# Expert weights ahead of the stage barrier, choice rounds moved, and a closing norm with ACT's square root, in an encoder kernel

## The reference

```python
tokens = rms_norm(x, norm_g).reshape(n_tok, d)
logits = jnp.einsum('nd,de->ne', tokens, w_router)
affinity = jax.nn.softmax(logits, axis=-1)
gate, idx = lax.top_k(affinity.T, cap)        # each of 16 experts takes 32 prompt, 128 sample tokens
xe = tokens[idx]
hid = silu(xe @ w_gate) * (xe @ w_up)         # per expert, 1024 x 1024 matrices
ye = (hid @ w_down) * gate
out = zeros.at[idx].add(ye)
y = rms_norm(x + out, final_g)
```

## Time and profile before

| | |
|---|---|
| median of 3 runs | 1362.23 us (1359.22, 1362.23, 1362.28) |
| the profiled execution | 1361.18 us, span 1359.5 us |
| TensorE busy | 1281.0 us, 94% |
| TensorE weight loads | 1116.0 us, 82% |
| VectorE busy | 916.3 us, 67% |
| ACT busy | 706.1 us, 52% |
| GpSimd busy | 306.1 us, 23% |
| mean granted TensorE clock | 0.969 |
| read from HBM, written | 274.41 MB, 39.44 MB |

### The profile page before, as it was taken

One profiled execution on the slowest core, in us unless ns is written; L12 is line 12 of the kernel. 1 busy time (PEld: TensorE's weight loads), 2 busy tenths in 40 slices (PEclk: granted clock), 3 DMA queues, 4 the chain that ended last, 5 costly groups with the idle time before them and its releaser, 6 DMA issues.

```text
span 1359.5 us, 24950 instructions
## 1 busy us (share of the span) xinstructions
PE 1281.0 (94%) x9744; PEld 1116.0 (82%) x9744; DVE 916.3 (67%) x1336; ACT 706.1 (52%) x1025; POOL 306.1 (23%) x304
## 2 busy tenths in 40 slices
PE   8999999999998999924999999999999999999992
PEld 7889999888897888814888888988898888988891
DVE  5363122341475555597988888888988888888976
ACT  6345221102244444215766677666766677666762
POOL 1122121010042222012141322223131322223030
PEclk8999999999999999966999999999999999999996
DMA  8022454342157774219799999999999999999994
GB/s 288 32 74 77 124 173 148 102 128 46 68 198 229 196 202 156 78 70 370 253 325 333 304 316 319 335 310 302 317 321 331 300 317 319 336 309 304 298 364 187
DMA packets 242030, 314.74 MB, mean 232 GB/s; under 512 B 16096, under 2 KB 206048, under 8 KB 241968
## 3 DMA queue, kind: packets, MB, share of 16 engines
q1 hardware_dynamic: 226576, 268.54, 59.9%
q0 software_dynamic: 15392, 45.36, 11.4%
HBM read 274.41 MB, written 39.44 MB: 231 GB/s over the span
## 4 chain that ended last, share of the span: by engine, by line
PE 90%; DVE 5%; DMA 2%; issue 1%; SPq 1%; ACT 1%; POOL 0%; ACTq 0%; DVEq 0%; POOLq 0%
PE psum L1860 26%; PE psum L1937 22%; PE psum L1944 10%; PE psum L1960 8%; PE psum L1750 7%; PE psum L1978 4%; PE psum L1969 4%; PE psum L1930 1%; PE psum L1783 1%; PE psum L1796 1%; PE psum L1797 1%; PE psum L1706 1%; PE psum L1731 1%; DVE eraw L1678 1%; DVE GI L1309 1%
## 5 line engine op out<-in xcount | busy, mean ns | idle before, releaser
L1609 DVE TENSOR_TENSOR elo<-eraw,ehi 128x2048 bf16<-128x2048 f32 x192 | 433.4, 2284 | 2.1 <-ACT ehi L1057 1.1
L1057 ACT ACTIVATE ehi<-eraw 128x2048 fp32r<-128x2048 f32 x192 | 362.3, 1902 | 48.4 <-DMA eraw<-in_w_gate_dram 28.9
L1937 PE MATMUL psum<-xc,ehi 128*128 128x320 f32 x2048 | 332.4, 314 | 1.9 <-DVE xc L1614 1.9
L1937 PEld LDWEIGHTS psum<-xc,ehi 128*128 128x128 f32 x2048 | 304.2, 189 | 3.5 <-DVE xc L1614 2.3
L1944 PE MATMUL psum<-xb,elo 128*128 128x160 bf16 x2048 | 164.1, 233 | 0.0
L1622 DVE TENSOR_REDUCE gu<-psum 128x320 f32<-128x640 f32 x128 | 105.2, 822 | 83.4 <-PE psum L1944 83.1
L1944 PEld LDWEIGHTS psum<-xb,elo 128*128 128x128 bf16 x2048 | 138.8, 98 | 13.2 <-issue 0.2
L1860 PE MATMUL psum<-hn_hi,whi 128*128 128x512 f32 (+1 forms) x384 | 137.3, 358 | 0.0
L1860 PE MATMUL psum<-hn_lo,whi 128*128 128x512 f32 (+1 forms) x384 | 136.1, 354 | 0.0
L1860 PE MATMUL psum<-hn_hi,wlo 128*128 128x512 f32 (+1 forms) x384 | 135.8, 354 | 0.0
L1960 PE MATMUL psum<-ehi,hc 128*128 128x512 f32 x512 | 132.6, 406 | 0.0
(11 more groups left out here) (253 smaller groups left out, 1978.8 us busy)
## 6 DMA issues: line engine op xcount, KB each, us to landing
eraw<-in_w_gate_dram SPq DMA_DIRECT2D x64, 1024.0 KB, 9.7
eraw<-in_w_up_dram SPq DMA_DIRECT2D x64, 1024.0 KB, 10.7
eraw<-in_w_down_dram SPq DMA_DIRECT2D x64, 1024.0 KB, 12.5
wraw<-in_w_in_dram SPq DMA_DIRECT2D x12, 1024.0 KB, 7.5
negm<-negm_d SPq DMA_DIRECT2D x10, 512.0 KB, 6.9
acc_d<-x POOLq DMA_DIRECT2D x10, 512.0 KB, 5.4
tok_d<-tk POOLq DMA_DIRECT2D x10, 512.0 KB, 3.0
v<-v_d SPq DMA_DIRECT2D x18, 256.0 KB, 4.3
```

The lines of the kernel that those rows point to most:

```text
L1057: act.activation(f["ehi"][:, j % RING, :], f["eraw"][:, raw_slot(s, j), :], ACT.Copy).then_inc(S["ehi"], 1)
L1609: dve.tensor_tensor(f["elo"][:, j % RING, :], f["eraw"][:, raw_slot(s, j), :], f["ehi"][:, j % RING, :].bitcast(F32), ALU.subtract).then_i ...
L1937: pe.matmul(o[:, 0:2 * NC], hi[:, k, c], x[:, k, :, :].rearrange("p a t -> p (a t)"), start=(k == 0), stop=False, skip_group_check=True)
```

## The change

- **Weights.** SP arrives at the barrier without waiting. The first expert's loads wait for the last output projection, and its down pieces (from piece 8 on, `RAW`) for the landing of the first gather's prompt part. That part now has its own semaphore `gath_p`, so the sample rows can be transposed before it lands.
- **Tokens of tile 7.** `LATE = NS - 1`: tile 7 now takes the way of tiles 8 and 9 over ACT and POOL. POOL starts these three multiplications when all ten affinity tiles are done. `g2b` has a place of its own, since the weights now land where it lay.
- **Choice rounds.** ACT copies the affinities to `AFF`. The rounds are laid 0, 1 to 3, 4 and 5, 6, 7, and then 8 to 11 after `arrive`.
- **Clock.** TensorE runs 48 transposes of the identity matrix after it has transposed the choice.
- **Closing norm.** For the second batch and for the last rows ACT takes the square root (with its table loaded by a first small root ahead of the second batch's sums), and VectorE forms the reciprocal and one Newton step (`polish`). Two of the second batch's six tiles are scaled after the last expert's rows are added. The prompt's last rows are finished and scattered first, waiting only for the prompt's plain stores, and the sample's second.

```diff
@@ -231,7 +231,7 @@
...
         d.update(overlay(at_stage, ("x1", [P, 2, D], F32)))
-        d.update(overlay(at_conv, ("tk", [P, 2, D], F32)))
+        d.update(overlay(at_conv, ("tk", [P, 2, D], F32), ("g2b", [P, D], F32)))
@@ -249,7 +249,7 @@
...
         og = d["og"][:, 2, SP_:T].rearrange("p (s n) -> p s n", s=2)
-        g2b = d["og"][:, 3, SP_:T]
+        g2b = d["g2b"][:, :]
@@ -294,8 +294,9 @@
...
         same_token = spare[:, 2 * D:2 * D + P]
-        fs = spare[:, 2 * D + P:2 * D + P + 3 * NT].rearrange("p (a n) -> p a n", a=3)
-        fl = spare[:, 2 * D + 2 * P:2 * D + 2 * P + 8].rearrange("p (a n) -> p a n", a=4)
+        fs = spare[:, 2 * D + P:2 * D + P + 4 * NT].rearrange("p (a n) -> p a n", a=4)
+        fl = spare[:, 2 * D + 2 * P:2 * D + 2 * P + 10].rearrange("p (a n) -> p a n", a=5)
+        eps = spare[:, 2 * D + 2 * P + 32:2 * D + 2 * P + 33]
         gains = colS[:, :, :].rearrange("p a c -> p (a c)")
@@ -381,6 +382,8 @@
...
+
+        LATE = NS - 1
@@ -546,9 +549,9 @@
...
             load_x(0)
-            sp.dma_start(g2b, rows_of(norm2_g)).then_inc(S["g2b_in"], 16)
             stored(staged[-1])
             load_mix(1)
+            sp.dma_start(g2b, rows_of(norm2_g)).then_inc(S["g2b_in"], 16)
             for n in range(2, NT + 1):
@@ -557,12 +560,18 @@
...
                     load_mix(n)
-            barrier(sp, 1)
+            arrive(sp)
...
                 for j in range(NB):
+                    if first and j == 0:
+
+                        sp.wait_ge(S["o_ps"], 2 * NT)
+                    if first and j == RAW:
+
+                        sp.wait_ge(S["gath_p"], 16)
                     if j >= RAW:
@@ -597,8 +606,8 @@
...
                 sp.wait_ge(S["f_y"], k + 1)
-                sp.dma_start(y_chunk[n], final_tile(n)).then_inc(S["f_out"], 16)
-            sp.wait_ge(S["f_out"], 16 * NT)
+                sp.dma_start(y_chunk[n], final_tile(n)).then_inc(S["f_out_p" if n < NTP else "f_out"], 16)
+            sp.wait_ge(S["f_out"], 16 * NS)
@@ -706,12 +715,13 @@
...
                     select_causal(n + 2)
-                if n >= 2 and not joint(m):
+                if n >= 2 and m < LATE:
                     pool.wait_ge(S["tk_done"], m + 1)
...
             pool.wait_ge(S["g2b_in"], 16)
-            for m in range(NS, NT):
-                pool.wait_ge(S["tk_scaled"], m - NS + 1)
+            pool.wait_ge(S["aff_done"], NT)
+            for m in range(LATE, NT):
+                pool.wait_ge(S["tk_scaled"], m - LATE + 1)
                 pool.tensor_tensor(d["tk"][:, m % 2, :], d["tk"][:, m % 2, :], g2b, ALU.mult
@@ -745,7 +755,7 @@
...
                                         bass.IndirectOffsetOnAxis(ap=idx[:, 1:2], axis=0)
-                                        ).then_inc(S["gath"], 16)
+                                        ).then_inc(S["gath_p"], 16)
@@ -792,6 +802,7 @@
...
                                     ).then_inc(S["f_gath"], 16)
+            pool.memset(eps, EPS)
             ch(pool.memset(same_token, 0.0))
@@ -801,15 +812,16 @@
...
             y_quarters = y_prompt[0].rearrange("t (j n) -> (t j) n", j=4)
-            pool.wait_ge(S["f_out"], 16 * NT)
+            pool.wait_ge(S["f_out_p"], 16 * NTP)
             pool.wait_ge(S["f_done"], 1)
+            settle()
+            pool.indirect_dma_start(y_quarters, bass.IndirectOffsetOnAxis(ap=f["idx"][:, 1, 1:2], axis=0),
+                                    f["yp"][:, :], None).then_inc(S["f_set"], 16)
+            pool.wait_ge(S["f_out"], 16 * NS)
+            pool.wait_ge(S["f_done"], 2)
             settle()
...
                                     f["yt"][:, :], None).then_inc(S["f_set"], 16)
-            pool.wait_ge(S["f_done"], 2)
-            settle()
-            pool.indirect_dma_start(y_quarters, bass.IndirectOffsetOnAxis(ap=f["idx"][:, 1, 1:2], axis=0),
-                                    f["yp"][:, :], None).then_inc(S["f_set"], 16)
             pool.wait_ge(S["f_set"], 32)
@@ -989,6 +1001,14 @@
...
+            def scaled_tokens(m):
+
+                act.wait_ge(tk_out[m % 2], 16 * (m // 2))
+                if not joint(m):
+                    act.wait_ge(S["lgmax"], m + 1)
+                act.activation(d["tk"][:, m % 2, :], d["x1"][:, m % 2, :], ACT.Copy, scale=d["ms"][:, m % 2, 1, H:H + 1]
+                               ).then_inc(S["tk_scaled"], 1)
+
@@ -1035,15 +1055,21 @@
...
                     columns_out(n - 1, 0)
+                if n == NT - 1:
+
+                    act.wait_ge(S["affT_ps"], 1)
+                    for i in range(NS // 4):
+                        act.activation(AFF[HALF2 * i:HALF2 * i + NE, :], psum[0:NE, (0, 4)[i], :], ACT.Copy
+                                       ).then_inc(S["aff_out"], 1)
                 if n < NT:
                     heads_high(n)
+                if n == NT - 1:
+                    scaled_tokens(LATE)
             for m in range(NS, NT):
...
             for m in range(NS, NT):
-                act.wait_ge(tk_out[m % 2], 16 * (m // 2))
-                act.activation(d["tk"][:, m % 2, :], d["x1"][:, m % 2, :], ACT.Copy, scale=d["ms"][:, m % 2, 1, H:H + 1]
-                               ).then_inc(S["tk_scaled"], 1)
-            barrier(act, 1)
+                scaled_tokens(m)
+            arrive(act)
@@ -1133,13 +1159,22 @@
...
             expert(NE - 1, 1, 3 * (NE // 2 - 1), last=True)
+            act.wait_ge(S["f_same"], 1)
+            act.activation(fs[:, 3, 0:1], eps, ACT.Sqrt)
             final_sums(*FINAL_BATCHES[1])
+            k0, k1 = FINAL_BATCHES[1]
+            act.wait_ge(S["f_sum"], k1)
+            act.activation(fs[:, 1, k0:k1], fs[:, 0, k0:k1], ACT.Sqrt, bias=eps).then_inc(S["f_root"], 1)
             act.wait_ge(S["f_row"], 1)
...
                            accum_out=fl[:, 0, 0:1]).then_inc(S["f_sq"], 1)
+            act.wait_ge(S["f_quart"], 1)
+            act.activation(fl[:, 1, 1:2], psum[:, 7, 0:1], ACT.Sqrt, bias=eps).then_inc(S["f_root"], 1)
+            act.wait_ge(S["f_sq"], 2)
+            act.activation(fl[:, 1, 0:1], fl[:, 0, 0:1], ACT.Sqrt, bias=eps).then_inc(S["f_root"], 1)
@@ -1316,7 +1351,10 @@
...
                         dve.wait_ge(x1_out[n % 2], 16 * (n // 2))
-                        dve.wait_ge(S["tk_done"], n - 1)
+                        if n - 2 < LATE:
+                            dve.wait_ge(S["tk_done"], n - 1)
+                        else:
+                            dve.wait_ge(S["tk_scaled"], 1)
                     else:
@@ -1523,7 +1561,7 @@
...
                 if n == NT:
-                    choose(both_halves, half, CAPS, 0, 2)
+                    choose(both_halves, half, CAPS, 1, 4)
                 if 1 <= n < NT:
@@ -1545,32 +1583,29 @@
...
-                    dve.wait_ge(S["affT_ps"], 1)
-                    for i in range(NS // 4):
-                        ch(dve.tensor_copy(AFF[HALF2 * i:HALF2 * i + NE, :], psum[0:NE, (0, 4)[i], :]))
+                    dve.wait_ge(S["aff_out"], NS // 4)
+                    choose(both_halves, half, CAPS, 0, 1)
                 if n == NT:
                     logit_peak(m)
-                    choose(both_halves, half, CAPS, 2, 4)
+                    choose(both_halves, half, CAPS, 4, 6)
                 if 2 <= n < NT - 1:
...
                     heads_low(n)
-                if n == NT - 1:
-                    tokens_out(m)
                 if n == NT + 1:
-                    choose(both_halves, half, CAPS, 4, 5)
+                    choose(both_halves, half, CAPS, 6, 7)
                     last_roots()
...
                     logit_bias(m)
-                    choose(both_halves, half, CAPS, 5, 6)
+                    choose(both_halves, half, CAPS, 7, 8)
                     affinities(m - 1)
...
             arrive(dve)
-            choose(both_halves, half, CAPS, 6, 12)
+            choose(both_halves, half, CAPS, 8, 12)
             dve.wait_ge(S["affT_ps"], 2)
@@ -1670,12 +1705,30 @@
...
             dve.wait_ge(S["gf_in"], 16 * 5)
-            for k0, k1 in FINAL_BATCHES:
-                dve.wait_ge(S["f_sum"], k1)
-                inverse_root(fs[:, 1, k0:k1], fs[:, 0, k0:k1], fs[:, 2, k0:k1])
+            def polish(r, v, t):
+
...
+
+                ch(dve.reciprocal(r, r))
+                ch(dve.tensor_tensor(t, r, r, ALU.mult))
+                ch(dve.scalar_tensor_tensor(t, t, -0.5, v, ALU.mult, ALU.mult))
+                ch(dve.scalar_tensor_tensor(r, t, 1.5, r, ALU.add, ALU.mult))
+
+            def scale_final(k0, k1):
+
...
+
+            (_, first), (_, _) = FINAL_BATCHES
+            dve.wait_ge(S["f_sum"], first)
+            inverse_root(fs[:, 1, 0:first], fs[:, 0, 0:first], fs[:, 2, 0:first])
+            scale_final(0, first)
+            dve.wait_ge(S["f_sum"], NT)
+            ch(dve.tensor_scalar(fs[:, 3, first:NT], fs[:, 0, first:NT], EPS, None, ALU.add))
+            dve.wait_ge(S["f_root"], 1)
+            polish(fs[:, 1, first:NT], fs[:, 3, first:NT], fs[:, 2, first:NT])
```

(25 more changed lines are left out.)

## The result

The changed kernel took **1405.2 us** (median of 4 runs, 1393.01 to 1409.22) against 1360.88 for the kernel before in the same session (4 runs): a ratio of 1.0311, 95% interval 1.0246 to 1.0376. It is slower by 44 us. The forecast was 1359.2 us in a range of 1351.5 to 1364; it was wrong. The profiled execution took 1405.34 (span 1403.6, mean granted clock 0.960).

The account below looks back on a forecast made before the run. The prediction took TensorE as the bound nearly everywhere, with a hole before the first expert's matmul. First matmul +1.0, clock -2.45 and tail -1.6 summed to -3.05, giving 1359.2 us on the median's scale, range 1351.5 to 1364.

Parts of the forecast that it names:

- The 15 experts after it are TensorE's and the change touches none of their work: Expert phase: every expert but the first stays at 43.82 us; only the hole before and the tail can move.
- the price of the 48 transposes: Between barrier and first matmul: the added TensorE transposes cost only their run time, 7.3 us.
- Choice rounds: Before the barrier on VectorE: 8 rounds instead of 6 end early, choice ready at 612.8 us instead of 617.8.
- GpSimd's path: Tiles 7 to 9 to the barrier: two store landings of 6.8 us and a 9.06 us drain, barrier open at 621.7.
- The rival of quiet stores: Token stores before the barrier land in 3.0 us each, barrier open at 614.1: -10.65, 1351.6 us; chance 0.18.
- The short drain: Rival: GpSimd's drain at the barrier takes 5.44 us, barrier open at 618.1: -6.65, 1355.6 us; chance 0.1.
- the two quotients: GpSimd's two drains in the kernel before: 82.3 and 82.4 ns for each DMA issued, so 9.06 us was kept.
- Barrier to first matmul: From barrier through the added transposes to first matmul: 11.3 us, so 633.0, 1.0 us later than before.
- The clock: First expert: the added transposes raise TensorE from 1.2 to 2.4 GHz, 43.8 us instead of 46.3, -2.45.
- the rival "if it only falls": The transposes lift the clock but it falls in the gap before the first matmul: 1361.6 us; no-clock rival's chance 0.14.
- The tail: After the last expert: shorter root, rows earlier, prompt's store first; 1.6 us off the end, bounds 0.3 and 2.5.
- my bound of 2.5: Upper bound of the gain after the last expert, in us, if the last store waits for VectorE alone.

Follow-up runs that it names:

- padding alone in both directions: Idle instructions ahead of TensorE's barrier: 96 added to the kernel before, 1407.61 us; 64 added to the whole change, 1358.31 us.
- the shortened body: The change without padding, its low products leaving out the first of eight parts in every expert but the first, 64 instructions fewer a pass: 1343.42 us.
- the last one with the gap filled: The change with tile 7 by VectorE, an early GpSimd drain, two splits ahead of the token splits, and TensorE's filler laid anew: 1347.94 us.
- the padded change: The whole change with 64 idle instructions (128 waits that are always met) added ahead of TensorE's barrier: 1358.31 us.
- 96 or 352 instructions: The kernel before with 96 or 352 idle instructions added ahead of TensorE's barrier: 1407.61 and 1429.36 us.
- 78: The kernel before with 78 idle instructions added ahead of TensorE's barrier: 1386.07 us.

## Why the prediction was wrong, step by step

- **The step that failed** is the sentence "The 15 experts after it are TensorE's and the change touches none of their work", and with it the price of the 48 transposes, which I set by the time that they run. Their work is untouched, but not where their code lies: 96 instructions ahead of the loop put it into an eighth block, and five of six jumps back cost a pass 8.3 to 10.4 us. In the trace that is +46.1 us, where the sum had nothing. It is shown by padding alone in both directions, by the period of 256, by the moving boundary and by the shortened body. No rival of mine held it.
- **Choice rounds, GpSimd's path, barrier.** Right. Choice ready at 613.9 (612.8), landings 6.63 (6.8), ACT's scaling 1.16 (1.1), drain 9.07 (9.06), barrier 622.4 (621.7). The rival of quiet stores is what the weights asked for late showed (2.96 us). The short drain did not come: 9.07 us for 110 DMAs and 5.44 at the end for 66, as the two quotients had it. (My steps to the last store add up to 605.55, not 605.75; the 0.2 us change nothing.)
- **Barrier to first matmul.** 633.06 for 633.0, but two misses cancel: the barrier opened 0.7 us later, and the way from it took 10.7 us and not 11.3. It led through VectorE's splits, not through the transposes; these took 7.05 us (6.8 to 8.0 in the variants, 7.3 forecast), and the token transposes behind them were done at 630.9. The two ways are close: with tile 7 by VectorE the chain leads through the transposes.
- **The clock.** This term failed too. The added transposes lift the clock and the gap loses it, the rival "if it only falls". Windows of TensorE in the changed kernel, and in the last one with the gap filled (us, busy (instructions), granted clock, DMA share, GB/s):

```profile
624.00:626.00 2.00, 2.00 (x12) 0.50 0.26 37
626.00:628.00 2.00, 2.00 (x19) 0.97 0.65 225
628.00:630.00 2.00, 2.00 (x21) 1.00 0.22 66
...
632.00:634.00 2.00, 0.94 (x4) 0.74 1.03 416
634.00:636.00 2.00, 2.00 (x9) 0.50 1.03 426
```

```profile
618.00:620.00 2.00, 2.00 (x19) 0.93 0.23 66
...
622.00:624.00 2.00, 2.00 (x18) 1.00 1.03 420
```

  In the changed kernel the clock goes from 1.2 to 2.4 GHz during the transposes and is back at 1.2 GHz at 634, after about 2 us without work. From the first matmul to the last row product the padded change takes 701.78 us and before 702.45, but the two kernels without the 48 transposes are as short, 701.91 (the change without them) and 701.67 (the tail alone). So the transposes gave nothing that these traces tell from zero, where I had -2.45, and the -0.7 isn't theirs; where it comes from was not tried. Filling the gap as well gave 1.55 us (700.23 for 701.78). I had weighed this gap and called it short.
- **The tail.** -1.6 forecast, -2.28 measured, within its bounds. The prompt's store goes out at 1392.9 and the sample's at 1394.4, 13.5 us behind TensorE's last row product; before, the second of the two went out 16.5 us behind it. At the drain behind them 2.3 of these 3.0 us are left (it begins at 1398.0, 17.1 us behind that product, and began at 1353.8, 19.3 behind), since the larger store, which took 3.4 us to land before against 2.6 of the other, is now the last. The sample's store had no plain store to wait for, only VectorE and the store ahead of it: that is the condition of my bound of 2.5.
- **The sum.** With the placement taken out the forecast of -3.05 stands against -3.7 (the change without its transposes) and -4.5 us (with padding), intervals of about 1.7 us to either side. That it comes so near is partly luck: the clock's -2.45 isn't in either, and in the changed kernel's trace the parts other than the five passes add up to -1.9. The mechanism of the choice, the stores, the barrier and the tail was right; 46 us lay in a part that I had put at nothing.

The slow layout isn't slow in every jump: five of six in the change and with 96 or 352 instructions, three of six with 78. In the pass behind the change's fast jump no code was fetched (none between 1235.0 and 1334.8 us), though the loop touches eight blocks there too: so eight can stay, and mostly don't. What decides in a single jump whether the block is still there stays open. The four executions of the change spread from 1393.01 to 1409.22 us, by more than one such jump costs; only one of them has a trace, so whether the number of slow jumps differs between them is not shown.

## What to carry to other kernels

Instructions added ahead of a hot loop cost more than their run time if the loop's code is near what TensorE can keep: count the loop's instructions, see how many blocks of 256 they touch, and look at the number of instruction fetches on the page and at "issue" at the loop's head; a few idle instructions of padding, or a shorter body, cure it. A change that comes out slower in a place that it doesn't touch should be run again with padding before any part of it is blamed. GpSimd's drain at the barrier went by the DMAs since the last one (9.07 us for 110, 0.31 for 4): pay it early, where GpSimd idles, and leave it more room than its DMAs suggest, as the added drains took 9.9 and 12.7 us for 106.

## What the runs showed of the hardware that I had not expected

- Seven blocks of 16 KB of loop code stay with TensorE from pass to pass (no fetch of code begins between 753 and 1297 us before); with eight, each of the five slow passes of the change fetches nine blocks again. The Trainium skill, "Advanced Engine Details and Errata" (ISA Cache), speaks of 128 KB on TensorE and, beside it, of only two lines of 16 KB; this loop of seven blocks ran without a fetch, so for TensorE the measurement decides against the two lines.
- The cost is waiting, not traffic: nine fetches are 0.15 MB in a pass. Those of the first slow jump, begun at 763.53, 763.57 and 772.37 us, took 1.67, 2.04 and 0.94 us. The record of the jump lasts 5.16 us, and TensorE's matmuls are idle for 2.05 us at it and for 5.46 at the second stall. What fills these times besides the fetches no record shows.
- Of the two added drains of GpSimd, both begun as a store was issued and with the same 106 DMAs to account for, the one at 571.3 took 9.9 us and the one at 586.2, beside the early weights, 12.7 us. Why was not tried.
